# Prompt attention over the memory in five turns a tile, with the queries turned into the bank of the value products

## The reference

```
h = h + mem_attend(rmsnorm(h, g_xattn), mem_k, mem_v)
    q = rmsnorm((hn @ w_xq) per head of 128, g_xq)       # 4 heads
    s = q k^T * 128 ** -0.5 ;  p = softmax(s)            # 256 memory rows
    o = p v ;  return o @ w_xo                           # 512 -> 1024
hn = rmsnorm(h, g_ffn)
logits = hn @ [w_rg | w_re] + [b_rg | b_re]              # 4 groups, 32 experts
```

## Time and profile before

| | before |
|---|---|
| median of three runs | 3746.19 us |
| the profiled execution: its own time | 3746.22 us |
| the profiled execution: span | 3744.7 us |
| TensorE (PE) busy | 3096.4 us, 83% of the span |
| VectorE (DVE) busy | 1880.6 us, 50% |
| ScalarE (ACT) busy | 1448.9 us, 39% |
| GpSimd (POOL) busy | 397.4 us, 11% |
| mean granted TensorE clock | 0.911 of full speed |

### The profile page before, as it was taken

The page is one execution under the profiler, slowest core; times in us unless marked ns, Lnnn a source line. Parts: engine busy times, 40 slices in busy tenths (PEclk is TensorE's granted clock), DMA queues, the critical chain, the costliest instruction groups (busy, mean ns, idle before and its releaser), DMA issues. The chain is left out here.

```text
span 3744.7 us, 62384 instructions
## 1 busy us (share of the span) xinstructions
PE 3096.4 (83%) x22834; PEld 2661.1 (71%) x22879; DVE 1880.6 (50%) x2768; ACT 1448.9 (39%) x2896; POOL 397.4 (11%) x397
## 2 busy tenths in 40 slices
PE   7999999899986999456599977886079999999970
PEld 7999999788875888434377755775067777778760
DVE  5243256455543555433266632332377777776734
ACT  5111354355554655312133223442055555554510
POOL 1000000000000000113000010111411111110113
PEclk9999999999997999767799987987589999999995
DMA  4333332234451121238233342322097887786849
GB/s 164 122 120 135 129 131 104 69 114 126 126 163 62 47 67 42 72 119 256 100 122 127 114 146 94 99 95 84 22 348 257 327 304 278 272 312 235 318 164 336
DMA packets 309901, 591.72 MB, mean 158 GB/s; under 512 B 80485, under 2 KB 136435, under 8 KB 309182
## 3 DMA queue, kind: packets, MB, share of 16 engines
q1 hardware_dynamic: 250798, 365.48, 29.8%
q0 software_dynamic: 47776, 196.29, 14.2%
q10 hardware_dynamic: 11136, 27.27, 2.0%
HBM read 462.07 MB, written 160.44 MB: 166 GB/s over the span
## 5 line engine op out<-in xcount | busy, mean ns | idle before, releaser
L136 PE MATMUL pj_pu<-pj_w,pj_nT 128*128 128x256 f32 (+3 forms) x1088 | 306.5, 282 | 0.0
L137 PE MATMUL pj_pu<-pj_w,pj_nT 128*128 128x256 f32 (+3 forms) x1088 | 305.7, 281 | 0.0
L138 PE MATMUL pj_pu<-pj_w,pj_nT 128*128 128x256 f32 (+3 forms) x1088 | 305.1, 280 | 0.0
L137 PEld LDWEIGHTS pj_pu<-pj_w,pj_nT 128*128 128x128 f32 (+1 forms) x1088 | 201.9, 186 | 0.0
L138 PEld LDWEIGHTS pj_pu<-pj_w,pj_nT 128*128 128x128 f32 (+1 forms) x1088 | 201.8, 185 | 0.0
L136 PEld LDWEIGHTS pj_pu<-pj_w,pj_nT 128*128 128x128 f32 (+1 forms) x1088 | 201.4, 185 | 0.1
L3102 ACT ACTIVATE ex_gate<-ex_gate_raw 128x2048 fp32r<-128x2048 f32 x64 | 119.1, 1909 | 209.0 <-DMA ex_gate_raw<-in_w_gate 124.8
L716 ACT ACTIVATE att_prob<-att_score,att_res 128x256 f32<-128x256 f32 (+1 forms) x384 | 127.6, 443 | 142.6 <-DVE att_res L752 142.6
L3156 DVE TENSOR_TENSOR ex_gate<-ex_gate_raw,ex_gate 128x2048 fp32r<-128x2048 f32 x64 | 143.8, 2288 | 74.0 <-ACT ex_gate L3102 62.0
L136 PE MATMUL pj_pu<-pj_nT,pj_w 128*128 128x384 f32 (+2 forms) x480 | 175.3, 365 | 0.0
L136 PE MATMUL ex_py<-ex_down,ex_hT 128*128 128x512 f32 x384 | 152.6, 397 | 26.0 <-DVE ex_hT L131 26.0
(11 more groups left out here) (566 smaller groups left out, 7944.4 us busy)
## 6 DMA issues: line engine op xcount, KB each, us to landing
ex_gate_raw<-in_w_gate SPq DMA_DIRECT2D x32, 2048.0 KB, 9.7
ex_up_raw<-in_w_up SPq DMA_DIRECT2D x32, 2048.0 KB
ex_down_raw<-in_w_down POOLq DMA_DIRECT2D x32, 2048.0 KB, 8.4
tmp_yb<-ex_y ACTq DMA_DIRECT2D x48, 512.0 KB, 7.1
out_win_k<-in_cache_k POOLq DMA_DIRECT2D x8, 2032.0 KB, 13.1
out_win_v<-in_cache_v POOLq DMA_DIRECT2D x8, 2032.0 KB, 14.4
tmp_att<-att_res POOLq DMA_DIRECT2D x48, 264.0 KB, 4.6
pout_att<-tmp_att SPq DMA_DIRECT2D x16, 792.0 KB, 7.4
```

What stands on the lines that cost most here:

```text
L136: pe.matmul(out, ah, bh, start=start, stop=False)
L137: pe.matmul(out, ah, bl, start=False, stop=False)
L138: return pe.matmul(out, al, bh, start=False, stop=stop)
```

## The change

The turn is put in another order on every engine but GpSimd, a tile passes through five turns (the logits of tile i - 4 stand in turn i), and the loop holds two turns: five turns are written out before it, five times two run in it, six are written out after it. The queries of the next tile are turned in the turn before, into the bank `V` of the value products; `turn_q` waits for the scaling of the rows there instead of for `pT`, and `turn_p` has the wait for `pT`. On ScalarE the copy of the queries comes behind the squares, and the root is a step of its own. The sample's rows have a buffer `oxs`, loaded at the start, as is the first `h1`. The waits that guard the shared banks are moved with the steps.

```diff
+        oxs = s.sb("oxs", [P, XW])
...
         def order(eng, turn):
-            for i in range(4):
+            for i in range(5):
                 turn(i)
-            with eng.Fori(4, PT) as i:
+            with eng.Fori(0, (PT - 6) // 2) as k:
+                turn(2 * k + 5)
+                turn(2 * k + 6)
+            for i in range(PT - 1, NT + 4):
                 turn(i)
-            for i in range(PT, NT + 3):
-                turn(i)
+        def later(step):
+            return lambda i: None if isinstance(i, int) and i == 0 else step(i)
...
                 q_load(0)
+                h1_load(0)
                 sp.dma_start(wr[:], ...)
-                order(sp, lambda i: each((prompt(q_load), i + 1), (h1_load, i - 1), (h2_store, i - 2), (hn_store, i - 2),
-                                         (sample_rows, i - 1), (lg_store, i - 3)))
+                sp.dma_start(oxs[:], t["ox"][PT]).then_inc(E["ox_in"], 16)
+                order(sp, lambda i: each((prompt(q_load), i + 1), (hn_store, i - 3), (h2_store, i - 2), (later(h1_load), i - 1),
+                                         (lg_store, i - 4)))
...
-                    act.activation(qT[:], v3(A[:, 0, :]), ACT.Copy).then_inc(E["qT_ok"], 1)
+                    act.activation(qT[:], v3(V[:, :]), ACT.Copy).then_inc(E["qT_ok"], 1)
...
-                order(act, lambda i: each((prompt(q_turned), i), (squares, i - 2), (prompt(exponentials), i), (h_turned, i - 3), (norm, i - 2)))
+                q_turned(0)
+                order(act, lambda i: each((prompt(exponentials), i), (squares, i - 2), (prompt(q_turned), i + 1), (root, i - 2),
+                                          (h_turned, i - 3), (norm, i - 2)))
...
-                order(dve, lambda i: each((residual, i - 2), (prompt(row_sums), i - 1), (prompt(maxima), i), (mean, i - 2), (prompt(attention), i - 1),
-                                          (norm, i - 2), (prompt(p_turned), i), (rows_turned, i - 1), (logits, i - 3)))
+                order(dve, lambda i: each((prompt(maxima), i), (prompt(attention), i - 1), (prompt(row_sums), i), (residual, i - 2),
+                                          (rows_turned, i - 1), (mean, i - 2), (prompt(p_turned), i), (logits, i - 4), (norm, i - 2)))
...
                 def turn_q(i):
                     pe.wait_ge(E["q_in"], i * 16 + 16)
-                    need(pe, E["pT_ok"], 2 * i)
+                    need(pe, E["ox_ok"], i - 1)
                     for h in range(XH):
-                        last = pe.transpose(A[:, 0, h * P:(h + 1) * P], q[:, h * P:(h + 1) * P], ident[:])
+                        last = pe.transpose(V[:, h * P:(h + 1) * P], q[:, h * P:(h + 1) * P], ident[:])
...
                 def out(i):
                     pe.wait_ge(E["oxT_ok"], i + 1)
-                    need(pe, E["lg_ok"], i - 1)
+                    need(pe, E["lg_ok"], i - 2)
+                    need(pe, E["hT_ok"], 2 * (i - 1))
...
                 def turn_p(i):
+                    need(pe, E["pT_ok"], 2 * i)
...
                 def logits(i):
+                    if isinstance(i, int) and i + 2 >= NT:
+                        pe.wait_ge(E["h2_ok"], 2 * NT)
+                    else:
+                        pe.wait_ge(E["h2_ok"], 2 * i + 5)
...
                 def turn_h(i):
                     pe.wait_ge(E["hn_ok"], i + 1)
                         pe.wait_ge(E["h2_ok"], 2 * i + 4)
+                        pe.wait_ge(E["oxT_ok"], i + 3)
...
+                turn_q(0)
-                order(pe, lambda i: each((prompt(turn_q), i), (out, i - 2), (prompt(scores), i), (turn_h, i - 3), (prompt(p_v), i - 1), (prompt(turn_p), i),
-                                         (turn_rows, i - 1), (logits, i - 3)))
+                order(pe, lambda i: each((prompt(scores), i), (prompt(p_v), i - 1), (out, i - 2), (turn_rows, i - 1), (prompt(turn_p), i),
+                                         (prompt(turn_q), i + 1), (logits, i - 4), (turn_h, i - 3)))
```

More of the change, by code:

```diff
@@ L2598, in h1_load @@
                     sp.dma_start(h1[:], t["h1"][i]).then_inc(E["h1_in"], 16)
[L2600 to L2603, removed]
                 def h2_store(i):
@@ L2728, in turn_q @@
                     pe.wait_ge(E["q_in"], i * 16 + 16)
-                    need(pe, E["pT_ok"], 2 * i)
+                    need(pe, E["ox_ok"], i - 1)
                     for h in range(XH):
-                        last = pe.transpose(A[:, 0, h * P:(h + 1) * P], q[:, h * P:(h + 1) * P], ident[:])
+                        last = pe.transpose(V[:, h * P:(h + 1) * P], q[:, h * P:(h + 1) * P], ident[:])
                     last.then_inc(E["q_turned"], 1)
-                def out(i):
-                    pe.wait_ge(E["oxT_ok"], i + 1)
-                    need(pe, E["lg_ok"], i - 1)
[L2737 to L2741, removed]
                 def scores(i):
@@ L2748, in scores @@
                     last.then_inc(E["score_ok"], 1)
[L2750 to L2759, removed]
                 def p_v(i):
                     need(pe, E["ox_ok"], i)
+                    pe.wait_ge(E["pT_ok"], 2 * i + 2)
                     for n in range(2):
-                        pe.wait_ge(E["pT_ok"], 2 * i + n + 1)
                         for m in range(4):
@@ L2769, in p_v, with out, turn_rows @@
                     last.then_inc(E["pv_ok"], 1)
+                def out(i):
+                    pe.wait_ge(E["oxT_ok"], i + 1)
+                    need(pe, E["lg_ok"], i - 2)
+                    need(pe, E["hT_ok"], 2 * (i - 1))
+                    for n in range(2):
+                        for h in range(XH):
+                            kk, cols = slice(h * P, (h + 1) * P), slice(512 * n, 512 * n + 512)
+                            last = matmul3(pe, X[:, n, :], oxT[:, 0, kk], oxT[:, 1, kk], wo[:, 0, h, cols], wo[:, 1, h, cols], h == 0, h == XH - 1)
+                    last.then_inc(E["xo_mm"], 1)
+                def turn_rows(i):
+                    rows = ox
+                    if isinstance(i, int) and i == PT:
+                        pe.wait_ge(E["ox_in"], 16)
+                        rows = oxs
+                    else:
+                        pe.wait_ge(E["ox_ok"], i + 1)
+                    need(pe, E["hT_ok"], 2 * (i - 2))
+                    for h in range(XH):
+                        last = pe.transpose(T[:, h * P:(h + 1) * P], rows[:, h * P:(h + 1) * P], ident[:])
+                    last.then_inc(E["ox_turned"], 1)
                 def turn_p(i):
+                    need(pe, E["pT_ok"], 2 * i)
                     for n in range(2):
@@ L2777, in turn_p @@
                         last.then_inc(E["p_turned"], 1)
[L2779 to L2788, removed]
                 def logits(i):
@@ L2797, in logits, with turn_h @@
                     last.then_inc(E["lg_mm"], 1)
+                def turn_h(i):
+                    pe.wait_ge(E["hn_ok"], i + 1)
+                    if isinstance(i, int) and i + 2 >= NT:
+                        pe.wait_ge(E["h2_ok"], min(2 * i + 4, 2 * NT))
+                        pe.wait_ge(E["oxT_ok"], NT)
+                    else:
+                        pe.wait_ge(E["h2_ok"], 2 * i + 4)
+                        pe.wait_ge(E["oxT_ok"], i + 3)
+                    for n in range(2):
+                        for k in range(4):
+                            last = pe.transpose((T[:, :], X[:, 1, :])[n][:, k * P:(k + 1) * P], hn[:, (4 * n + k) * P:(4 * n + k + 1) * P], ident[:])
+                        last.then_inc(E["h_turned"], 1)
                 pe.wait_ge(E["consts_in"], 80)
```

6 lines of the change are left out of this document (4 added, 2 removed).

## The result

The changed kernel took 3652.91 us (median of four runs, 3650.58 to 3656.18), the kernel before, beside it, 3743.43 us (3733.07 to 3754.71): a ratio of 0.9757, with an interval of 0.9735 to 0.9780. The forecast was 3663 with a range of 3645 to 3698. The profiled execution took 3650.58 us against 3746.22, 95.6 us less; its mean granted clock is 0.922 against 0.911.

The account below looks back on a forecast made before the run. The prediction took a loop of waits between TensorE and its two copying engines as the bound. Head, twelve turns of 13.90 us and tail made the stage 83.7 us shorter: 3746.22 to 3662.5, said as 3663, range 3645 to 3698.

Parts of the forecast that it names:

- The looped turn, 13.90: Attention stage's loop: TensorE waits for nothing, its tasks sum to 13.90 us a turn instead of 19.13.
- The head, 45.9 to turn 4: Stage's start: from first scores at 2267.68, turns 0 and 1 take 10.0 each, 2 and 3 12.7 and 13.2; turn 4 at 2313.6.
- The tail: Stage's end: 7.5 us of products, two output products behind waits, 16 to the last logits, 1.5 slower clock each; ends 2527.7.
- the forecast's chain through h2, the norm and the copy: Tail: each output product waits about 4.8 us for h2, the split, the turning of h and its copy.
- the tail's two clock terms: Tail: two output products at a falling clock, 1.5 us more each.
- A wait for the query copy: Looped turns: query copy behind the squares delays the scores, turn up to 16.2 us, 3677 to 3691 us; chance 0.14.
- The loop's return: Loop of two turns: each of five returns stalls 4.1 us for instruction fetch, 20 us, 3683 us; chance 0.04.
- The waits did not come back: Looped turns: TensorE's waits as before, in other places, turn 18.3 us, about 3736 us; chance 0.04.
- The clock did not fall: Looped turns: 4.64 us of small work or the shared bank lowers the clock, turn 27.8 us, 3850 us; chance 0.03.
- Paid twice: Looped turn of before: TensorE's waits cost 2.90 us idle, then 1.54 us of slower output product.

Follow-up runs that it names:

- loop of one turn: The changed kernel with one turn in its loop, run ten times, instead of two turns run five times: 3650.88 us, ratio 0.9740.
- one idle copy: The changed kernel with one unread 0.6 us copy on ScalarE ahead of the query copy, from the fifth tile on: 3644.05 us in one run.
- four turns: The changed kernel with logits of tile i - 3 behind the turning of h, so a tile passes through four turns instead of five: 3739.93 us, ratio 0.9988.
- the bank alone: The changed kernel with the queries turned back in the bank of the probabilities, new order kept: 3721.08 us, ratio 0.9943.
- VectorE's one line: The kernel before with VectorE's copies of the probabilities moved ahead of the norm's reciprocal: 3706.83 us, ratio 0.9900.
- four idle copies: The changed kernel with four unread copies on ScalarE ahead of the query copy, from the fifth tile on: 3661.63 us, ratio 0.9788.
- seven idle copies: The changed kernel with seven unread copies on ScalarE ahead of the query copy: 3703.22 us, ratio 0.9896.

## Why the prediction was right

The direction, the mechanism and the range held. The forecast's 3663 lies 10 us above 3652.9, which is at the lower edge of the forecast's own 3652 to 3676; the medians are 90.5 us apart, the profiled executions 95.6. Term by term, from the first scores on (343.7 us to the last logits before, 249.0 after, so 94.8 less where the sum had 83.7):

- **The looped turn, 13.90, was 13.49**: 0.41 us eleven times, 4.6. The tasks were right, but their starts were read from a turn with waits in it. The row of eight transposes of the probabilities takes 0.87 from start to start where I took 1.00, rows and queries 0.44 each (0.49 and 0.50), value products 1.71 (1.79), h 0.91 (0.94), scores 1.72 (1.75), output product 5.69 (5.72). This turn is the same, 13.48 to 13.50, in every trace whose looped turns have no wait.
- **The head, 45.9 to turn 4, was 44.1**: 1.9 us. Turns 0 and 1 took 9.42 and 9.10, not 10.0 each; turns 2 and 3 took 12.44 and 13.10, against 12.7 and 13.2. The loads added ahead of the first scores pushed nothing back: these stand 12.1 us after the first load, before 12.4.
- **The tail was 4.6 us shorter**, 43.2 us from the last value products to the last logits against 47.8: 3.0 for a clock that I let fall in its output products and that did not fall in this execution, as the rows below show (6.74 us from 2498.89 to the next logits, with a wait of 0.88 in it), 1.7 in the last stretch (14.3 us from the last sums to the last logits, against 16), and 0.2 for a slip, since the tail's terms add up to 2527.5 and not 2527.7 (a second slip, 5.9 for 5.8 us between 2351.2 and 2357.0, touches no term). The stretch up to the last sums took 0.4 longer.

TensorE in time, the last two output products and what follows, after:

```profile
2488.27 0.48 PE L136 MATMUL mx_X<-mw_wo,mx_oxT 128*128 128x512 f32 x1 [0.89 <-ACT mx_hT L2665]
...
2498.89 0.48 PE L136 MATMUL mx_X<-mw_wo,mx_oxT 128*128 128x512 f32 x1 [0.89 <-ACT mx_hT L2665]
...
2512.74 1.11 PE L2812 MATMUL mx_T<-mx_ident,mx_hn 128*128 128x128 f32 x4 [1.47 <-POOL mx_hn L2633]
...
2515.44 3.60 PE L2799 MATMUL mx_X<-mx_wr,mx_hT 128*128 128x36 f32 x16 [0.73 <-issue]
```

The waits of 0.89 are the forecast's chain through h2, the norm and the copy; the transposes and logits slow down only at the very end, behind TensorE's wait of 1.47 for GpSimd's `hn`. VectorE, the last sums and the last logits, against the earlier trace rows:

```profile
2504.79 1.29 DVE L2687 TENSOR_TENSOR mx_h<-mx_X,mx_h 128x512 f32<-128x512 f32 x2 [7.51 <-PE mx_X L138]
...
2519.07 0.20 DVE L2726 TENSOR_TENSOR mx_lg<-mx_X,mx_br 128x36 f32<-128x36 f32 x1 [7.57 <-PE mx_X L2799]
```

Head and tail are less certain than the turn. In the traces of the loop of one turn and of one idle copy the head to turn 4 took 45.1 us and the tail 45.1 to 45.2: there the last output product did run at a lower pace (TensorE in time, loop of one turn: 8.26 us from its start to the next logits, against 6.74):

```profile
2495.03 0.62 PE L136 MATMUL mx_X<-mw_wo,mx_oxT 128*128 128x512 f32 x1 [0.89 <-ACT mx_hT L2664]
...
2503.29 1.95 PE L2798 MATMUL mx_X<-mx_wr,mx_hT 128*128 128x36 f32 x16 [0.88 <-DVE mx_h L2686]
```

So one of the tail's two clock terms came in those executions, and that neither came here is the luck of one execution. Luck, too, is that the one turn of the earlier trace rows stands for the mean: turns 4 to 14 of before took 18.5 to 20.2 us, 19.12 in the mean, and their waits were 1.6 to 2.9 us.

**The rivals.** A wait for the query copy did not come, and when it was put there the looped stretch lost 1.3 us a turn at 1.03 us of wait. The loop's return costs nothing at one turn or at two. The waits did not come back. The clock did not fall in the 4.4 us of transposes and logits in one piece (2417.71 to 2422.07 and its like in each turn). Nor does the bank that queries and value products share bring the clock down: it is used so in every looped turn at 1.00, while the run with the queries in the other bank had 0.86, and 0.98 once its wait was filled. That rival named a behaviour that exists, but of the waits: in the four kernels whose looped turns held 2.5 to 2.9 us of waits in the mean, the granted clock was 0.84 to 0.88.

**Paid twice.** The prediction read before as 2.90 us of waits and 1.54 of slower output product. Both halves are shown: filling the waits in before brings the output product back to 5.72, and lengthening one wait in the changed kernel from 1.03 to 2.6 us takes the scores from 1.99 to 3.77. My expectations for four turns, for the bank alone and for VectorE's one line missed for the same reason, counting a wait once or little more. Side by side, idle time of TensorE and length of one looped turn, and the granted clock from 2320 to 2480 us:

| kernel | idle, us | turn, us | clock |
|---|---|---|---|
| changed | 0 | 13.49 | 1.00 |
| four idle copies | 1.03 | 14.80 | 1.00 |
| before, copies of the probabilities first | 1.86 (two turns 1.56) | 16.37 (two turns 19.0) | 0.96 (1.00 in a turn of 16.37, 0.82 in one of 19.0) |
| seven idle copies | 2.60 | 18.4 | 0.88 |
| before, the turn of the earlier trace rows | 2.90 (2.5 in the mean of turns 4 to 14) | 19.13 (mean 19.12) | 0.87 |
| queries in the bank of the probabilities | 2.89 | 19.35 | 0.86 |
| four turns | 2.93 | 20.0 | 0.84 |

Not shown is what a wait between these lengths costs in the changed kernel, and whether several short waits cost as much as one long one: the row with 1.86 has its waits in another order of work than the rows around it, and no run spread the same wait over one order. Nor does a run undo ScalarE's new order alone.

## What to carry to other kernels

Where TensorE and its copying engines wait for each other in turn, look for the wait that a shared buffer or an early place in the order makes, and give the steps one turn more and a bank that is free then; both were needed here, since with either one undone a quarter of the gain (the bank) or next to nothing (the fifth turn) was left. Where waits of TensorE of the size met here, 2.6 to 2.9 us in a turn, stand in such a loop, price them at about twice their length, as these runs showed it, and read the rows behind it as well as the idle time. Take start-to-start durations from a stretch where the engine doesn't wait, and try single moved lines first: one line of VectorE's order was worth 35 us.

## What was not expected of the hardware

Idle transposes made a kernel faster. 24 of them, 2.78 us, in a wait of 2.9 us shortened the turn from 19.35 to 16.60 us, because the matmuls behind the wait ran at the full clock again; 18 spread over the waits of before took 1.5 us off its turn. And of two waits in one place, the one of 1.03 us left the granted clock of the looped stretch at 1.00, and the one of 2.6 us took it to 0.88. With the same three waits ahead, 1.56 us together, the clock fell in two turns of one run and stayed at full speed in others of the same loop.
